# Two transformer blocks on one core: norms joined to the residual ahead of them and the dense stage behind them

## The chip, the core and the metric

One core of a Trainium2 chip runs the whole program. The metric is the time of one execution on the device, in microseconds (us). The five engines have an instruction stream each: TensorE (PE, its weight loads PEld), VectorE (DVE), ScalarE (ACT), GpSimd (POOL) and SyncE (SP, which here only issues loads). All numbers are f32, so a 128x128 by 128x512 matmul takes TensorE two passes, and the trace counts two instructions for it.

## The reference, cut to what matters

```python
def rmsnorm(x, g):
    y = x32 * lax.rsqrt(jnp.mean(x32 * x32, axis=-1, keepdims=True) + EPS)
    return (y * g.astype(jnp.float32)).astype(x.dtype)

def modulate(x, g, shift, scale):
    return rmsnorm(x, g) * (1 + scale) + shift
```

The first block (512 latent and 256 context tokens of width 1024) is: modulated norm, projections, a chunked state-space scan, its output times silu(z) and normed over 2048 features, windowed attention, a gated merge of both, `w_out`, and a feed-forward part with a depthwise convolution (`w_up`, `w_down`); then a final norm. The second block has four layers (SGU, RWKV, MLA, SGU). Each adds `gate * mixer(h)` to x, with `h = rms_norm(x) * (1 + scale) + shift`; the first two also update the context. MLA norms its ranks: `q = rms_norm(c_q, q_norm) @ w_uq`, and likewise `c_kv` for latent and context tokens.

## The kernel before

Features lie on the partitions, tokens along the free axis: x is 8 tiles of 128 features by 512 tokens (`A_XL`) and 8 by 256 (`A_XC`). Weights come tile by tile through two slots; SP issues the load of a tile as soon as TensorE has released its slot (`slot_used`), also across stages.

The program is a list of stages. `program` walks it on each engine: before stage n an engine waits until all four compute engines have finished stage n-1 (`eng.wait_ge(chip.stage_done, 4 * n)`, line 3814), then runs its own part. That is the barrier. POOL also clears the semaphores of every other stage there. `Joined` runs two stages as one, without a barrier; before, three norms are joined to the dense stage behind them (`norm_in` with `Xbc`, two layer norms with `SguValues`, one with the q projection).

`Norm` (line 643) works in four steps. ScalarE squares each tile (line 666). TensorE adds the squares over partitions and tiles with a matrix of ones (line 683), one matmul for each tile of 128 features, and then runs 8 filler matmuls (`keep_busy`, line 691; 3 where `norm.busy = 3`). ScalarE takes the root (line 669). VectorE takes the reciprocal (line 704) and scales each tile (line 707), and ScalarE adds the shift (line 675).

The stages around the change, in order (34 barriers in all):

- `GateZ` (line 1173): 16 products with `w_z`. ScalarE takes silu, VectorE multiplies y (line 1216) and then does a part of the modulation's products beside it (`SideModulation.reduce`, line 632, on weights `w_side` that POOL loads). `LoadContext` on SP waits for the stage barrier and loads the second block's context, ahead of the loads of `w_qkv`. Norm of y over 2048 features. `Attention` (line 1224): four projections into banks 0 to 3, then the values, then rotation and heads. `Merge` reads the normed y.
- `StrassenResidual` (line 1575): x += gate * (w @ y) with seven products of half-size blocks in place of eight, four passes of seven. `w_out1`, then a norm, then `FfnUp` (line 1691), which begins with sums of blocks of weights (`a_sum`) and of h (`b_sum`) on VectorE.
- `Residual` for `w_down` (line 1538, 8 steps of 22 matmuls), the final norm, the first layer's norm, `SguValues` (line 1876).
- `w_sgu_out`, norm, `RwkvFeatures` (line 2693), which needs differences of neighbouring tokens of the whole h before its first product.
- `w_rwkv_out`, norm, three projections to the MLA ranks (`Project`, line 2251, copies on line 2286), a norm of the ranks, `Mla` (line 2302).
- `w_mla_out`, norm, `SguValues`.

Of the kernel before, what the change touches and what calls it, by code (L numbers as in the profile page):

```python
# [20 lines left out]
P = 128  # L21
# [401 lines left out]
class Joined:  # L423


    def __init__(self, chip, first, make_second):
        self.first = first
        chip.joining = True
        self.second = make_second(first)
        chip.joining = False  # L430
        self.index = first.index

    def sync(self, sp):
        self.first.sync(sp)
        self.second.sync(sp)

    def tensor(self, pe):
        self.first.tensor(pe)
        self.second.tensor(pe)

    def scalar(self, act):
        self.first.scalar(act)
        self.second.scalar(act)

    def vector(self, dve):
        self.first.vector(dve)
        self.second.vector(dve)

    def gpsimd(self, pool):
        self.first.gpsimd(pool)  # L450
        self.second.gpsimd(pool)
# [191 lines left out]
class Norm(Stage):  # L643


    def __init__(self, chip, name, jobs, work):
        super().__init__(chip)
        self.jobs, self.work = jobs, work
        self.squared, self.summed, self.rooted, self.scaled, self.shifted = (
            chip.sem(f"{name}_{s}") for s in ("squared", "summed", "rooted", "scaled", "shifted"))  # L650
        self.busy = 8

    def places(self):

        at = self.work
        for n, job in enumerate(self.jobs):
            k, t = job["x"].shape[1:]
            yield job, n, self.chip.view(at, k, t), self.chip.view(at, t), self.chip.view(at + t, t), \
                self.chip.view(A_SMALL + 32 * n, k), k, t
            at += k * t  # L660

    def scalar(self, act):
        a = self.nc.scalar
        for job, n, squares, rms, inv, factor, k, t in self.places():
            for i in range(k):
                a.activation(squares[:, i], job["x"][:, i], ACT.Square).then_inc(self.squared, 1)  # L666
        for job, n, squares, rms, inv, factor, k, t in self.places():
            act.wait_ge(self.summed, n + 1)
            a.activation(rms, self.chip.bank(n, t), ACT.Sqrt, scale=1.0 / (k * P), bias=EPS).then_inc(self.rooted, 1)
        done = 0  # L670
        for job, n, squares, rms, inv, factor, k, t in self.places():
            if job.get("shift") is not None:
                for i in range(k):
                    act.wait_ge(self.scaled, done + i + 1)
                    a.activation(job["out"][:, i], job["out"][:, i], ACT.Identity, bias=job["shift"][:, i:i + 1]).then_inc(self.shifted, 1)
            done += k

    def tensor(self, pe):
        done = 0
        for job, n, squares, rms, inv, factor, k, t in self.places():  # L680
            for i in range(k):
                pe.wait_ge(self.squared, done + i + 1)
                last = self.nc.tensor.matmul(self.chip.bank(n, t), self.chip.const("ones"), squares[:, i], start=(i == 0), stop=(i == k - 1))  # L683
            last.then_inc(self.summed, 1)
            done += k
        self.keep_busy()

    def keep_busy(self):

        for i in range(self.busy):  # L690
            self.nc.tensor.matmul(self.chip.bank(7), self.chip.const("ones"), self.chip.view(A_CONST, 512), start=True, stop=True)

    def vector(self, dve):
        v = self.nc.vector
        for job, n, squares, rms, inv, factor, k, t in self.places():
# [3177 lines left out]
```

## Time and profile before

| what | us |
|---|---|
| median of 3 runs (5244.01 to 5247.77) | 5244.16 |
| profiled execution | 5238.18 |
| its span | 5236.4 |
| PE busy in it | 4717.6 (90%) |
| DVE busy | 2623.1 (50%) |
| ACT busy | 1226.9 (23%) |
| POOL busy | 661.0 (13%) |
| mean granted clock of TensorE | 0.954 |

The span is the time from the first to the last instruction of the profiled execution; 1.8 us of that execution lie around it. The granted clock is a share of TensorE's full 2.4 GHz. In a row of a timeline, "x16" counts the instructions that were merged, and the brackets give the engine's idle time ahead of it and what ended that.

### The profile page before, as it was taken

What the parts mean: (1) busy time and instruction counts of PE and PEld (TensorE: products, weight loads), DVE (VectorE), ACT (ScalarE), POOL (GpSimd) and SP (SyncE); (2) the same over time, 40 slices, a digit from 0 to 9 for tenths busy, and PEclk for the clock granted to TensorE, in tenths of its full rate; (3) what the DMA queues carried; (4) which work ended last, traced back from release to release, by engine and by line L of the source; (5) the groups of instructions that cost most, each with busy time, mean ns of one, the idle gap of its engine ahead of it and who ended that gap; (6) DMA issues with size and microseconds to landing.
All of it is one profiled execution on the core that took longest, in us unless ns stands there. A gap on an engine that the chain in (4) does not pass through costs nothing.

```text
span 5236.4 us, 72681 instructions
## 1 busy us (share of the span) xinstructions
PE 4717.6 (90%) x29212; PEld 3011.0 (58%) x29212; DVE 2623.1 (50%) x4628; ACT 1226.9 (23%) x2254; POOL 661.0 (13%) x894
## 2 busy tenths in 40 slices
PE   7987798989999989999989856899898999999998
PEld 3555645544578434555545545789644555455687
DVE  2457754655588222334476486455624444333465
ACT  2223312420011010111010164223112444301230
POOL 0014400000000000110000041655000000000000
PEclk9999999989999999999989966999999999999999
DMA  4322150034322211223112266344211001021222
GB/s 149 102 83 81 61 177 29 31 131 156 106 73 81 75 54 41 99 100 107 36 48 99 101 214 217 91 113 114 67 45 49 29 35 37 21 93 65 73 85 81
DMA packets 152504, 451.27 MB, mean 86 GB/s; under 512 B 73200, under 2 KB 73456, under 8 KB 130800
## 3 DMA queue, kind: packets, MB, share of 16 engines
q1 hardware_dynamic: 128464, 350.91, 19.8%
q0 software_dynamic: 22848, 92.29, 5.1%
q8 instruction: 233, 3.82, 0.3%
q10 hardware_dynamic: 864, 3.47, 0.2%
q14 instruction: 95, 0.78, 0.0%
HBM read 377.42 MB, written 69.21 MB: 85 GB/s over the span
## 4 chain that ended last, share of the span: by engine, by line
PE 60%; issue 10%; DVE 9%; PEld 8%; POOLq 5%; ACT 2%; DMA 2%; DVEq 2%; POOL 1%; PEldq 0%; SPq 0%; ACTq 0%
PE psum L389 44%; PEld psum L389 7%; PE psum L1906 5%; POOLq L2905 2%; POOLq L2903 2%; PE psum L2275 1%; PE psum L683 1%; PE psum L2463 1%; PE psum L2464 1%; DVE sbuf L1156 1%; DVE sbuf L704 1%; PE psum L2435 1%; PE psum L1094 1%; DVE sbuf L2610 1%; DVE sbuf L707 1%
## 5 line engine op out<-in xcount | busy, mean ns | idle before, releaser
L389 PE MATMUL psum<-sbuf 128*128 128x256 f32 (+3 forms) x9328 | 2938.9, 474 | 109.4 <-DVE sbuf L1657 32.7
L389 PEld LDWEIGHTS psum<-sbuf 128*128 128x128 f32 (+1 forms) x9328 | 1757.1, 190 | 1247.9 <-issue 915.1
L3515 PE MATMUL psum<-sbuf 64*64 64x64 f32 (+1 forms) x10752 | 425.9, 238 | 29.7 <-SPq L3424 18.1
L3515 PEld LDWEIGHTS psum<-sbuf 64*64 64x64 f32 x10752 | 412.2, 138 | 46.2 <-SPq L3424 19.8
L1906 PE MATMUL psum<-sbuf 128*128 128x512 f32 x640 | 280.1, 599 | 15.7 <-ACTq L1913 8.6
L632 DVE CUSTOM_DVE_ANT_0 sbuf<-sbuf 128x1024 f32<-128x1024 f32 x160 | 196.2, 1226 | 135.1 <-DMA sbuf<-w_side 99.7
L1906 PEld LDWEIGHTS psum<-sbuf 128*128 128x128 f32 x640 | 122.6, 192 | 173.1 <-issue 172.1
L1669 DVE SCALAR_TENSOR_TENSOR sbuf<-psum,sbuf 128x256 f32<-128x256 f32 (+2 forms) x288 | 125.9, 480 | 189.9 <-PE psum L389 184.8
L3640 ACT ACTIVATE sbuf<-psum 128x256 f32<-128x256 f32 (+3 forms) x384 | 128.5, 368 | 363.8 <-PE psum L3515 302.2
L666 ACT ACTIVATE sbuf<-sbuf 128x512 f32<-128x512 f32 (+1 forms) x114 | 53.0, 551 | 598.4 <-DVEq L3814 581.2
L2904 POOL TENSOR_TENSOR sbuf<-sbuf 96x30 f32<-96x30 f32 (+14 forms) x240 | 138.3, 576 | 50.9 <-issue 18.1
L622 POOL DMA_DIRECT2D sbuf<-w_side x128 | 68.4, 535 | 592.9 <-DVE sbuf L632 567.1
L1932 DVE TENSOR_TENSOR sbuf<-sbuf 128x512 f32<-128x512 f32 x40 | 27.8, 694 | 226.1 <-ACT sbuf L1922 226.1
L2902 POOL TENSOR_TENSOR sbuf<-sbuf 96x30 f32<-96x30 f32 (+14 forms) x240 | 131.0, 546 | 33.0 <-issue 0.9
L3745 DVE TENSOR_SCALAR sbuf<-psum,sbuf 128x64 f32<-128x64 f32 x192 | 45.7, 280 | 148.3 <-PE psum L3515 147.0
L1657 DVE TENSOR_TENSOR sbuf<-sbuf 128x1024 f32<-128x1024 f32 (+1 forms) x100 | 100.2, 1006 | 31.1 <-DMA sbuf<-w_sgu_out 12.2
L683 PE MATMUL psum<-sbuf 128*128 128x512 f32 (+1 forms) x228 | 94.0, 570 | 22.9 <-ACT sbuf L666 22.9
L2610 DVE TENSOR_REDUCE sbuf<-psum 128x1 f32<-128x768 f32 x64 | 61.2, 956 | 106.4 <-PE psum L2464 106.0
L589 POOL DMA_DIRECT2D sbuf<-cond_rows x4 | 2.4, 603 | 874.5 <-DVEq L3814 815.9
L2806 DVE TENSOR_TENSOR sbuf<-sbuf,psum 128x384 f32<-128x384 f32 x128 | 66.7, 553 | 78.5 <-PE psum L389 75.8
L720 DVE TENSOR_SCALAR sbuf<-sbuf 128x512 f32<-128x512 f32 (+1 forms) x68 | 36.3, 533 | 138.2 <-ACT sbuf L850 136.1
L2463 PE MATMUL psum<-sbuf 128*128 128x512 f32 (+1 forms) x256 | 104.4, 489 | 0.0
(329 smaller groups left out, 5244.5 us busy)
## 6 DMA issues: line engine op xcount, KB each, us to landing
sbuf<-w_side POOLq DMA_DIRECT2D x128, 512.0 KB, 3.9
sbuf<-w_sgu_uz SPq DMA_DIRECT2D x32, 1088.0 KB, 5.0
sbuf<-terms SPq DMA_DIRECT2D x115, 256.0 KB, 2.8
sbuf<-w_up SPq DMA_DIRECT2D x22, 1024.0 KB, 5.0
sbuf<-w_merge SPq DMA_DIRECT2D x8, 2560.0 KB, 8.9
sbuf<-w_mla_head SPq DMA_DIRECT2D x16, 1152.0 KB, 5.1
sbuf<-w_sgu_v SPq DMA_DIRECT2D x8, 2048.0 KB, 7.9
sbuf<-w_sgu_out SPq DMA_DIRECT2D x8, 2048.0 KB, 8.2
```

Of the source, the lines that this page charges most:

```text
L389: last = nc.tensor.matmul(out, w, x, start=(n == 0), stop=(n == len(pairs) - 1))
L632: last = v.tensor_tensor_reduce(junk, self.slot[b], self.rows[:, c], 1.0, 0.0, ALU.mult, ALU.add, self.sums[:, b, n:n + 1])
L683: last = self.nc.tensor.matmul(self.chip.bank(n, t), self.chip.const("ones"), squares[:, i], start=(i == 0), stop=(i == k - 1))
L1669: last = v.scalar_tensor_tensor(x[:, m], self.chip.bank(i)[:, cols], gates[sign][:, m:m + 1], x[:, m], ALU.mult, ALU.add)
L1906: last = self.nc.tensor.matmul(self.chip.bank(x % 4), h[:, k, at:at + P], w[:, k], start=(k == 0), stop=(k == KD - 1))
L2463: t.matmul(s[:, a:a + w], self.qn[u][:, q], self.kn[u][:, a:a + w], start=True, stop=False)
L2610: v.tensor_reduce(self.mx[:, n:n + 1], self.s_bank(n), AX.X, ALU.max)
L2902: engine.tensor_tensor(product, left, right, ALU.mult)
L2903: eng.drain()
L2904: engine.tensor_tensor(x[:, j + 1:BLK, 0:j], x[:, j + 1:BLK, 0:j], product, ALU.add)
L3515: last = t.matmul(out[hs], lhs[hs], rhs[hs], start=start, stop=stop)
L3640: copy = lambda to, of: a.activation(to, of, ACT.Copy)
```

## The change

`Joined` takes any number of stages. Six joined groups replace 21 stages: gate, context load, norm and attention; `w_out1`, norm and `FfnUp`; `w_down`, final norm, new context, layer norm and `SguValues`; `w_sgu_out`, norm and `RwkvFeatures`; `w_rwkv_out`, norm, the three projections and the norm of the ranks; `w_mla_out`, norm and `SguValues`. The number of barriers falls from 34 to 19.

A norm now has a host, the stage ahead of it, and its work is cut in rows (one tile of latent features, or one of latent and one of context). TensorE adds a row's squares between the host's products as soon as the row is final (`sum_row`); what is left comes behind them (`last_sums`), then 8 fillers. ScalarE squares a row when the host says it is done (`next_row`), after loading the root's table. The norm of y has no fillers, takes bank 3, and its last sums stand behind the attention's first projection. In front of `SguValues` the latent half is scaled in four blocks of 128 tokens. `few` keeps the squares in two buffers, where room is short. Two of the first weight sums of `FfnUp` stand between the scalings. The context load waits for the start of its stage, which is now the gate's.

```diff
@@ class Joined @@
-    def __init__(self, chip, first, make_second):
-        self.first = first
+    def __init__(self, chip, make):
+        self.index = chip.begin_stage()
         chip.joining = True
-        self.second = make_second(first)
+        self.parts = make()
         chip.joining = False
...
@@ class Norm @@
+    def next_row(self, act, r):
+        for n, m in self.rows[r]:
+            self.host.row_done(act, n, m)
+        if self.few and r >= 2:
+            act.wait_ge(self.taken, r - 1)
+        self.square_row(act, r, [self.jobs[n]["x"][:, m] for n, m in self.rows[r]])
+    def sum_row(self, pe, r):
...
+            pe.wait_ge(self.squared, at + 1)
...
+            last = self.nc.tensor.matmul(self.chip.bank(self.banks[n], t), self.chip.const("ones"), self.square(r, n, m),
+                                         start=first, stop=at == self.last[n])
...
+        if self.host:
+            a.activation(self.chip.view(A_SMALL + 500, 1), self.chip.const("ones")[:, 0:1], ACT.Sqrt)
+            for r in range(self.started, len(self.rows)):
+                self.next_row(act, r)
...
+    def pieces(self):
+        for n, (k, t) in enumerate(self.sizes):
+            blocks = self.blocks if n == 0 else 1
+            for b in range(blocks):
+                for i in range(k):
+                    yield n, self.jobs[n], i, slice(t // blocks * b, t // blocks * (b + 1)), i == 0
...
+        if not self.placed:
+            self.last_sums(pe)
+            self.keep_busy()
...
@@ class GateZ @@
                 products(self.nc, self.chip.bank(u), [(w[:, k], self.h[:, k]) for k in range(KD)]).then_inc(self.w.used(u), 1)
+                if 2 * i + u >= 2:
+                    self.norm.sum_row(pe, 2 * i + u - 2)
...
                 self.nc.scalar.activation(self.z[u], self.chip.bank(u), ACT.Silu).then_inc(self.activated, 1)
+                if 2 * i + u >= 1:
+                    self.norm.next_row(act, 2 * i + u - 1)
...
@@ class Attention @@
-        for n in range(4):
+        pe.wait_ge(self.gate.activated, KS + 1)
+        project(0, 0, 0)
+        self.norm.last_sums(pe)
+        pe.wait_ge(self.gate.activated, KS + 2)
+        for n in range(1, 4):
+            if n == 3:
+                pe.wait_ge(self.norm.rooted, 1)
+                pe.wait_ge(self.norm.scaled, 1)
             project(0, n, n)
...
         act.dma_start(self.mask, c.dram["win_mask"]).then_inc(self.tables_in, 16)
+        act.wait_ge(self.norm.scaled, 1)
         act.dma_start(self.wv.rearrange("p k m -> p (k m)"), c.dram["w_att_v"]).then_inc(self.wv_in, 16)
...
@@ class Residual @@
+                if self.norm and 2 * i + u >= 1:
+                    self.norm.sum_row(pe, 2 * i + u - 1)
...
@@ class StrassenResidual @@
+    ROWS = (4, 0, 5, 1, 6, 2, 7, 3)
+    def row_done(self, eng, n, m):
+        eng.wait_ge(self.added, 7 * (m % (KD // 2)) + (7 if m < KD // 2 else 6))
...
+                if self.norm and p == KD // 2 - 1 and i >= 1:
+                    if i == 1:
+                        pe.wait_ge(self.added, 7 * p + 1)
+                    self.norm.sum_row(pe, i - 1)
...
@@ class FfnUp @@
+                    if j == 0:
+                        pe.wait_ge(self.norm.shifted, self.HALF * (S.B_PLAIN[n][0] + 1))
...
+    def first_sums(self, dve, i):
+        if i == self.HALF - 1:
+            self.a_sum(dve, 0, 2)
+        if i == KD - 1:
+            self.a_sum(dve, 0, 5)
...
             first, second, op = S.B_SUMS[n]
+            dve.wait_ge(self.norm.shifted, KD)
...
@@ class SguValues @@
-                    if (i, u, t) == (0, 0, 0):
-                        pe.wait_ge(self.norm.shifted, k + 1)
+                    if (i, u) == (0, 0) and t < 4:
+                        pe.wait_ge(self.norm.shifted, KD * t + k + 1)
...
@@ class Project @@
+            if self.rank and self.row + 2 * i + u >= 1:
+                self.rank.sum_row(pe, self.row + 2 * i + u - 1)
...
@@ class RwkvFeatures @@
-        for h, at, n in self.parts:
+        for h, at, n in reversed(self.parts):
+            dve.wait_ge(self.norm.shifted, KD if n == TL else 2 * KD)
...
@@ block1, sgu_layer, rwkv_layer, mla_layer @@
+    def attention():
+        gate, load = GateZ(chip, side), LoadContext(chip)
+        norm = Norm(chip, "norm_ssd", [dict(x=y, out=y, gain=chip.vec("ssd_g"))], None, host=gate, by_host=KS - 2, started=KS - 1, banks=[3],
+                    few=dict(slots=[ATT, ATT + TL], roots=[ATT + 2 * TL]), turn=2, placed=True)
+        return [gate, load, norm, Attention(chip, gate, norm)]
...
+    def down():
+        residual = Residual(chip, "w_down", KF, lambda k: g[:, k], part(5, 0))
+        norm = Norm(chip, "norm_out", [dict(x=x_lat, out=x_lat, gain=chip.vec("final_g"))], FFN_G + KF * TL,
+                    rows=[[(0, m)] for m in range(KD)], host=residual, by_host=KD - 1, banks=[7], turn=2)
+        return [residual, norm, NewContext(chip, load)]
...
+    def projected():
+        stages = before()
...
+        return stages + [norm, q, kv, Project(chip, "w_mla_rope", 1, both, chip.view(KROPE, 1, T), previous=kv), rank]
```

TensorE around the end of the gate's products, before (L389 are products of a dense stage, L683 sums of squares, L691 fillers):

```order
L389 MATMUL psum<-sbuf 128x512 x128
L683 MATMUL psum<-sbuf 128x512 x16
L691 MATMUL psum<-sbuf 128x512 x8
L389 MATMUL psum<-sbuf 128x512 x24
L389 MATMUL psum<-sbuf 128x256 x56
```

and now (L714 sums of squares), from the sum behind the 13th of the 16 gate products on:

```order
L714 MATMUL psum<-sbuf 128x512
L389 MATMUL psum<-sbuf 128x512 x8
L714 MATMUL psum<-sbuf 128x512
L389 MATMUL psum<-sbuf 128x512 x8
L714 MATMUL psum<-sbuf 128x512
L389 MATMUL psum<-sbuf 128x512 x8
L714 MATMUL psum<-sbuf 128x512
L389 MATMUL psum<-sbuf 128x512 x8
L714 MATMUL psum<-sbuf 128x512 x2
L389 MATMUL psum<-sbuf 128x512 x16
L389 MATMUL psum<-sbuf 128x256 x56
```

The 16 sums stood in one block behind the gate. Now one follows each of the gate's products from the third on, and the last two follow the attention's first projection; the fillers are gone.

TensorE from `w_down` to the SGU values (L1906), before:

```order
L389 MATMUL psum<-sbuf 128x512 x176
L683 MATMUL psum<-sbuf 128x512 x8
L691 MATMUL psum<-sbuf 128x512 x8
L683 MATMUL psum<-sbuf 128x512 x8
L683 MATMUL psum<-sbuf 128x256 x8
L691 MATMUL psum<-sbuf 128x512 x3
L1906 MATMUL psum<-sbuf 128x512 x192
```

and now, from the sum behind the sixth step of `w_down` on (L761 fillers, L2043 values):

```order
L714 MATMUL psum<-sbuf 128x512
L389 MATMUL psum<-sbuf 128x512 x22
L714 MATMUL psum<-sbuf 128x512
L389 MATMUL psum<-sbuf 128x512 x22
L714 MATMUL psum<-sbuf 128x512 x2
L761 MATMUL psum<-sbuf 128x512 x8
L714 MATMUL psum<-sbuf 128x256 x8
L714 MATMUL psum<-sbuf 128x512 x8
L761 MATMUL psum<-sbuf 128x512 x8
L2043 MATMUL psum<-sbuf 128x512 x192
```

Of the final norm's eight sums six lie between the products, one behind the last one, and one waits for its result. The layer norm adds the context first, and has 8 fillers in place of 3.

TensorE from `w_rwkv_out` to the MLA ranks (projections are L2275), before:

```order
L389 MATMUL psum<-sbuf 128x384 x112
L683 MATMUL psum<-sbuf 128x512 x8
L683 MATMUL psum<-sbuf 128x256 x8
L691 MATMUL psum<-sbuf 128x512 x3
L2275 MATMUL psum<-sbuf 128x512 x56
L2275 MATMUL psum<-sbuf 128x256 x8
L2275 MATMUL psum<-sbuf 128x512 x8
L2275 MATMUL psum<-sbuf 128x256 x8
L2275 MATMUL psum<-sbuf 128x512 x8
L2275 MATMUL psum<-sbuf 128x256 x8
L683 MATMUL psum<-sbuf 128x512 x8
L683 MATMUL psum<-sbuf 128x256 x2
L691 MATMUL psum<-sbuf 128x512 x8
```

and now, from the first of the two `w_mla_kv` products on (projections are L2430):

```order
L2430 MATMUL psum<-sbuf 128x512 x8
L2430 MATMUL psum<-sbuf 128x256 x8
L714 MATMUL psum<-sbuf 128x512
L2430 MATMUL psum<-sbuf 128x512 x8
L2430 MATMUL psum<-sbuf 128x256 x8
L714 MATMUL psum<-sbuf 128x512
L714 MATMUL psum<-sbuf 128x256
L2430 MATMUL psum<-sbuf 128x512 x8
L2430 MATMUL psum<-sbuf 128x256 x8
L714 MATMUL psum<-sbuf 128x512
L714 MATMUL psum<-sbuf 128x256
L761 MATMUL psum<-sbuf 128x512 x8
```

The sums of the ranks' squares stand one product behind, and only the last row and the fillers follow the third projection.

## Rows read from the trace of the kernel before

**Rows 1.** The page, part 1: TensorE's and the other engines' busy time.

```profile
PE 4717.6 (90%) x29212; PEld 3011.0 (58%) x29212; DVE 2623.1 (50%) x4628; ACT 1226.9 (23%) x2254; POOL 661.0 (13%) x894
```

**Rows 2.** Stretches: us, length, busy of five engines (instructions), granted clock, DMA share, GB/s.

```profile
760.70:801.00 40.30, 23.47 (x49) 9.95 (x48) 20.40 (x29) 10.90 (x19) 0.10 (x1) 0.80 0.30 117
1430.80:1450.50 19.70, 14.02 (x33) 6.01 (x33) 10.24 (x13) 11.51 (x18) 0.00 (x0) 1.00 0.17 53
1890.00:1933.90 43.90, 29.77 (x70) 14.05 (x71) 23.58 (x31) 22.08 (x44) 0.00 (x0) 0.86 0.13 48
1933.90:1943.40 9.50, 9.49 (x17) 4.23 (x18) 0.00 (x0) 1.71 (x3) 0.00 (x0) 0.75 0.00 0
2628.70:2667.70 39.00, 17.52 (x50) 9.05 (x49) 29.37 (x32) 18.93 (x36) 0.00 (x0) 0.80 0.04 13
3837.20:3860.60 23.40, 13.22 (x39) 7.12 (x39) 14.65 (x22) 15.94 (x34) 0.00 (x0) 0.92 0.08 23
...
4770.00:4788.10 18.10, 9.72 (x22) 4.09 (x23) 9.40 (x11) 10.89 (x18) 0.00 (x0) 0.92 0.32 116
```

**Rows 3.** Timeline, ACT: the gate's last two silus and the fourth projection's eviction.

```profile
753.88 0.60 ACT L1207 ACTIVATE sbuf<-psum 128x512 f32<-128x512 f32 x1 [6.28 <-PE psum L389]
760.76 0.60 ACT L1207 ACTIVATE sbuf<-psum 128x512 f32<-128x512 f32 x1 [6.28 <-PE psum L389]
...
827.62 0.38 ACT L1374 ACTIVATE sbuf<-psum 128x256 f32<-128x256 f32 x1 [2.87 <-PE psum L389]
```

**Rows 4.** Timeline, gate stage: a silu, a reduction and the multiply behind it.

```profile
725.89 1.23 DVE L632 CUSTOM_DVE_ANT_0 psum<-sbuf 128x1024 f32<-128x1024 f32 x1 [0.64 <-DMA sbuf<-w_side]
726.36 0.60 ACT L1207 ACTIVATE sbuf<-psum 128x512 f32<-128x512 f32 x1 [6.28 <-PE psum L389]
...
728.76 0.69 DVE L1216 TENSOR_TENSOR sbuf<-sbuf 128x512 f32<-128x512 f32 x1
```

**Rows 5.** The tile `w_qkv`: its four loads.

```profile
DMA to landing us min/median/max: 6.4/7.5/11.4
```

**Rows 6.** Timeline, PE: the layer norm's sums and the first SGU values.

```profile
1909.56 13.18 PE L683 MATMUL psum<-sbuf 128*128 128x512 f32 x32 [3.94 <-ACT sbuf L666]
...
1933.91 31.40 PE L1906 MATMUL psum<-sbuf 128*128 128x512 f32 x67 [8.59 <-ACTq L1913]
```

**Rows 7.** Timeline, same place: reciprocals and scalings on DVE, first eviction on ACT.

```profile
1899.42 3.35 DVE L704 RECIPROCAL sbuf<-sbuf 128x512 f32<-128x512 f32 x1 [8.26 <-ACT sbuf L669]
1902.85 5.39 DVE L707 SCALAR_TENSOR_TENSOR sbuf<-sbuf 128x512 f32<-128x512 f32 x8
...
1928.68 1.75 DVE L704 RECIPROCAL sbuf<-sbuf 128x256 f32<-128x256 f32 x1
...
1943.42 0.60 ACT L1922 ACTIVATE sbuf<-psum 128x512 f32<-128x512 f32 x1 [7.79 <-PE psum L1906]
```

**Rows 8.** Timeline, start of `FfnUp`: first sums of h, second weight tile.

```profile
1450.87 3.49 DVE L1785 TENSOR_TENSOR sbuf<-sbuf 128x1024 f32<-128x1024 f32 x3
...
1464.80 5.42 PE L389 MATMUL psum<-sbuf 128*128 128x256 f32 x24 [0.26 <-issue]
```

**Rows 9.** Timeline, RWKV layer: sums, reciprocal, first vector work, first product.

```profile
2630.20 10.61 PE L683 MATMUL psum<-sbuf 128*128 128x512 f32 x32 [1.48 <-ACT sbuf L666]
...
2638.17 3.35 DVE L704 RECIPROCAL sbuf<-sbuf 128x512 f32<-128x512 f32 x1 [8.34 <-ACT sbuf L669]
...
2652.69 2.28 DVE L2776 TENSOR_TENSOR sbuf<-sbuf 128x2032 f32<-128x2032 f32 x1 [0.70 <-ACTq L3814]
...
2667.68 2.90 PE L2830 MATMUL psum<-sbuf 128*128 128x512 f32 x4 [20.00 <-DVE sbuf L2760]
```

**Rows 10.** Timeline, norm of the ranks: first reciprocal, and MLA's first load.

```profile
3945.26 3.35 DVE L704 RECIPROCAL sbuf<-sbuf 128x512 f32<-128x512 f32 x1 [6.51 <-ACT sbuf L669]
...
3960.25 0.34 ACTq L2488 DMA_DIRECT2D sbuf<-rope_mla  x1
```

**Rows 11.** Timeline, ACT: first eviction of the last layer's SGU values.

```profile
4797.30 0.60 ACT L1922 ACTIVATE sbuf<-psum 128x512 f32<-128x512 f32 x1 [7.28 <-PE psum L1906]
```

More of the change, by code:

```diff
@@ new lines, in row_done, with square, sums_done, square_row @@
+    def row_done(self, eng, n, m):
+        if n == 0:
+            eng.wait_ge(self.scaled, m + 1)
+    def square(self, row, n, m):
+        if self.few:
+            k, t = self.sizes[n]
+            return self.chip.view(self.few["slots"][row % 2] + (0, self.sizes[0][1])[n], t)
+        return self.squares[n][:, m]
+    def sums_done(self, eng, n):
+        eng.wait_ge(self.summed, 1 + sum(last < self.last[n] for last in self.last))
+    def square_row(self, act, r, sources):
+        for (n, m), x in zip(self.rows[r], sources):
+            self.nc.scalar.activation(self.square(r, n, m), x, ACT.Square).then_inc(self.squared, 1)
@@ L662, in scalar @@
     def scalar(self, act):
         a = self.nc.scalar
[L664 to L669, printed above, removed]
+        if self.host:
+            a.activation(self.chip.view(A_SMALL + 500, 1), self.chip.const("ones")[:, 0:1], ACT.Sqrt)
+            for r in range(self.started, len(self.rows)):
+                self.next_row(act, r)
+        elif self.by_host == 0:
+            for r, row in enumerate(self.rows):
+                self.square_row(act, r, [self.jobs[n]["x"][:, m] for n, m in row])
@@ L670, in scalar @@
+        for n, (k, t) in enumerate(self.sizes):
+            self.sums_done(act, n)
+            a.activation(self.rms[n], self.chip.bank(self.banks[n], t), ACT.Sqrt, scale=1.0 / (k * P), bias=EPS).then_inc(self.rooted, 1)
         done = 0
-        for job, n, squares, rms, inv, factor, k, t in self.places():
+        for n, job, i, cols, _ in self.pieces():
+            done += 1
             if job.get("shift") is not None:
+                act.wait_ge(self.scaled, done)
+                a.activation(job["out"][:, i, cols], job["out"][:, i, cols], ACT.Identity, bias=job["shift"][:, i:i + 1]).then_inc(self.shifted, 1)
@@ L678, in tensor @@
     def tensor(self, pe):
[L679 to L686, printed above, removed]
+        if not self.placed:
+            self.last_sums(pe)
+            self.keep_busy()
@@ L1854, in block1, with ffn, inputs @@
     g = chip.view(FFN_G, KF, TL)
-    return [
+    def ffn():
+        out1 = StrassenResidual(chip, "w_out1", merged, [(x_lat, part(2, 0), TL)], A_WORK, A_HL)
+        norm = Norm(chip, "norm_ffn", [dict(x=x_lat, out=h_lat, gain=g2, scale=part(4, 0), shift=part(3, 0))], A_WORK + KD // 2 * 5 * TL // 2,
+                    rows=[[(0, m)] for m in out1.ROWS], host=out1, by_host=6, banks=[7], turn=1)
+        return [out1, norm, FfnUp(chip, norm)]
+    def inputs():
+        norm = Norm(chip, "norm_in", [job_lat, job_ctx], A_WORK)
+        return [norm, Xbc(chip, side, norm)]
@@ L1873 @@
+    return stages, down
 SGU_V = A_WORK
```

223 lines of the change are left out of this document (140 added, 83 removed).

## The prediction, before the changed kernel was run

> **What bounds the kernel now.** I read the page first: TensorE is busy 90% of the span [rows 1]. So only its idle stretches, its slow stretches and its filler products can be saved. I then cut the span at the places where the changed kernel joins stages, one stretch for each, from the end of the last product ahead of a norm to the first one behind it [rows 2]. The reader is to see two things there: each stretch is long (18 to 44 us), and the granted clock is under 1 in most of them and in the 9.5 us behind one (0.75), so the first products after a norm run partly at 1.2 GHz. The timeline of the engine that ends a stretch gives the times inside it [rows 3, 6 to 11]. I call the end of the last product E. A product of eight 128x512 matmuls takes 6.88 us at full clock, the step between two evictions [rows 3], so 0.86 us for one matmul and 0.43 for 128x256. Eight filler matmuls of `keep_busy` take 6.9.
>
> **What the change does, in general.** The sums of squares (one 0.86 us matmul per 128 rows of features) are not removed. Most move into the product loop ahead, where TensorE has no gap, so each costs its full time there; I charge all of them to the path. What goes is the barrier, the wait for squares, the idle time behind the fillers and the slow restart. Fillers: eight in every late norm, against three before in three norms.
>
> **1. Gate, norm, attention.** Before, the fourth of the attention's projections is evicted at 827.62, 66.9 us after E = 760.7 [rows 2, 3]; between lie vector reductions that finish late, 16 sums, 8 fillers, a wait for the scalings and a slow restart (clock 0.80 over the stretch). Now the projections need only free banks; the norm of y is read two stages later. Path: 16 sums 13.8, projections 3 x 6.88 + 3.44 = 24.1, eviction 0.3: 38.2. **Gain 28.7.** The last projection waits for the root (bank 3), which comes about 13 us before it is needed. The reciprocal and 16 scalings (3.4 and 16 x 0.67 = 14.1 us by the rates of [rows 7]) lie beside projections and values. If that cover were missing, VectorE's rotation would be late; it has some 20 us of spare, since the values follow. Behind the new ScalarE wait for `scaled` stand the load of the value weights and the four copies; the load is issued some 12 us before it is used. On SP the context load no longer waits for the gate's end and holds up nothing behind it; on POOL only the clearing of semaphores between stages falls away.
>
> **2. w_out1, norm, w_up.** Now, from E: 8 sums 6.9 (the last row's squares come within the two sums ahead of it), root 0.9, reciprocal 3.4, eight scalings 5.4 [rows 7] and two weight sums 1.4 between them, shift 0.7: the first sum of h starts at E + 18.7, against 1450.87 - 1430.8 = 20.1 [rows 8]. Then 13.9 us passed until the second weight tile's products [rows 8], 12.1 of them seven products of 1.73. Two of these (3.5) now run before the sum; the rest waits for VectorE's sums. This is worth 0 to 3.5; I take 3.0, since VectorE's sums take only 7.6 of the 13.9. **Gain 4.4**, bounds 1 to 6.
>
> **3. w_down, norm, norm, SGU values.** Before, the first values are evicted at 1943.42, 53.4 us after E = 1890.0 [rows 7]. Now: eight sums with a short wait for the last row 7.8, 8 fillers 6.9, 8 context sums 3.4, 8 latent sums 6.9, 8 fillers 6.9: 31.9. The chain beside it (root, reciprocal, scaling, squares, root, reciprocal of 128 columns, first shift) is ready at 27.5, so the fillers set the time. Reciprocals took 3.35 for 512 and 1.75 for 256 columns [rows 7]; for 128 I take 0.9, between 0.8 and 1.75, hidden either way. Plus 6.88 + 0.2: 39.0. **Gain 14.4**, bounds 11 to 16.5.
>
> **4. w_sgu_out, norm, RWKV features.** Here the first product needs the whole norm and 14 us of vector work. Before, the reciprocal starts at E + 9.5 and the first product is 29.5 later [rows 9]. Now all 16 sums are on the path: the latent ones end at 9.9, root 0.9, reciprocal at 10.9, then the same chain less one barrier, 0.7 [rows 9]: 39.7, against 39.0. **Loss 0.7**, bounds -3 to +1.5. The row's 20.00 us of idle time stays.
>
> **5. w_rwkv_out, norm, three projections, norm, MLA.** Before, MLA's first load is issued at 3960.25, 123.1 us after E = 3837.2 [rows 10]. Now: 16 sums 10.3, fillers 6.9, so q starts at 17.2 (its input is ready at 15.7; before 23.4 [rows 2] and slow). Projections 72.2 (six of 6.88, three of 10.32), seven rank rows 6.5: 95.9. Then copies and roots 1.8, and 15.0 from the first reciprocal to the barrier [rows 10]: 112.7. **Gain 10.3**, bounds 8 to 12.5.
>
> **6. w_mla_out, norm, SGU values.** Before, first eviction at 4797.30, 27.3 after E = 4770.0 [rows 11]. Now 8 sums 6.9, fillers 6.9, product 6.88, 0.2: 20.9. **Gain 6.4**, bounds 4 to 8.
>
> **The sum.** 28.7 + 4.4 + 14.4 - 0.7 + 10.3 + 6.4 = 63.5 us. The profiled execution took 5238.2 (span 5236.4); that gives 5174.7. The median of the runs shown is 6.0 above it, so I predict 5180.7. A 0.2% step, 10.5 us, is what a measurement of this kernel can tell from no change.
>
> **A rule weighed.** The restarts credited above are some 2 us each: behind the SGU norm, after 3.94 and 8.59 us of idle time [rows 6], the clock was 0.75 for 9.5 us [rows 2], and the first eviction came 2.4 us later than 6.88 + 0.2. About as much stands in parts 1 (2.3), 5 (1.7) and 6 (2.1); without them the gain would be 8.5 smaller. The Trainium skill, page TensorE: Matmul & The Clock Gate, Part 1, says that "the default state is throttled, and activity releases the throttle". By that rule the added fillers are worth having; by the rows they cost up to 4.2 us each where the input is ready first (part 6: input at 9.6, fillers end at 13.8). I go by the rows: fillers are charged in full, and the restart is free behind them.
>
> **Rivals.**
> - **Each hosted row costs more than its matmul.** 65 sums stand alone between accumulations into other banks. At a pass's seam TensorE stood 0.26 us idle [rows 8]. At that price for each: 17 us, gain 46.5, 5198. For it: every such sum has a wait of its own. Against: the squares are there long before, and 16 that follow each other took 10.6 us, 0.3 over 8 x (0.86 + 0.43) [rows 9].
> - **Loads lose their cover.** The attention's first weights (1536 KB, 6.4 to 11.4 us to landing [rows 5]) were loaded beside the norm. Now they have 8.6 us, with a 1 MB context load just ahead. At worst 3 us there, and a few us more where w_sgu_v's second tile comes late: 5185.
> - **The gate loop turns into a chain, slower than before.** ScalarE now squares row k-1 behind silu k and waits for VectorE's multiply, which stands behind a reduction that waits for w_side. If that multiply comes over 5.7 us after its silu (ScalarE's 6.28 us of idle time [rows 3] less a 0.55 us square), the next silu and then TensorE stall. With all else gained it needs over 4.5 us more in each of 14 steps to pass the time before; with 5 us it would be 5251. The largest lag seen was 2.4 us (728.76 behind 726.36 [rows 4]). So it is far from its point, and longer steps ease the loads. The page Perfetto Trace Analysis of the Trainium skill, Per-instruction lifecycle, calls ACT and DVE strict FIFO; by that rule nothing behind the waiting square can pass it, and the trace agrees in that VectorE's multiply starts only behind the reductions, with no idle time of its own [rows 4].
> - **The joined stages end no sooner.** If another engine ended them (VectorE in 2 to 4), only part 1 would count: 5215.
>
> **How the numbers follow.** Forecast 0.77 (5170 to 5192), costly rows 0.11, loads 0.05, no sooner 0.02, no effect within 0.2% 0.03, chain 0.02. All of the bounds at their worst give a gain of 47, at their best 75: 5169 to 5197. I widen both ends by a few us for the median and the costly rows: 5166 to 5202. Faster by over 0.2%: 0.95; within: 0.03; slower: 0.02.
>
> **What would show it.** The fourth projection evicted 27 us behind the gate's last product (38.2 less the 13 sums that now stand ahead of it); first SGU evictions without a slow pass (steps of 6.88 from the start); the 20 us wait of the RWKV features still there, some 2 us longer; MLA's first load 113 us after E, hosted sums included. Wrong would be: idle TensorE inside the gate loop, sums of over 1 us each, a wait on w_qkv, or a granted clock under 1 behind the fillers.

## The result, and the profile after

The changed kernel takes 5190.27 us in the median of four runs (5182.09 to 5194.39), the kernel before, beside it, 5244.97 (5244.01 to 5247.77). The ratio is 0.9897, with a 95% interval of 0.9882 to 0.9911: 54.7 us faster, where 63.5 was forecast. The profiled execution took 5182.09, 56.1 less than the profiled one of before. The forecast of 5180.7 (5166 to 5202) holds the time, but the sum behind it is not as good as that looks: two of its terms did not come, and gains outside the change's own places stood in for them.

The page's first part, after, answers to [rows 1]:

```profile
span 5180.3 us, 72699 instructions
PE 4703.1 (91%) x29226; PEld 3006.8 (58%) x29226; DVE 2631.4 (51%) x4682; ACT 1240.5 (24%) x2309; POOL 660.3 (13%) x894
```

To see which part gave what, I measured the same stretch in both traces, from one instruction to another that exist in both kernels (us):

| part | from, to | before | after | gain | forecast |
|---|---|---|---|---|---|
| 1 | first silu of the gate, attention's swaps | 191.0 | 162.0 | 29.0 | 28.7 |
| 2 | w_out1's first weight sum, w_down's last addition (5.2 of hosted sums taken off) | 512.0 | 506.3 | 5.7 | 4.4 |
| 3 | w_down's last addition, first eviction of the values (the same 5.2 put on) | 53.4 | 53.4 | 0.0 | 14.4 |
| 4 | w_sgu_out's first weight sum, first product of the features | 189.3 | 189.3 | 0.0 | -0.7 |
| 5 | w_rwkv_out's first weight sum, MLA's first load | 199.6 | 189.7 | 9.9 | 10.3 |
| 6 | w_mla_out's first weight sum, first eviction of the values | 128.8 | 131.1 | -2.3 | 6.4 |

These add up to 42.3. The other 13.8 lie where the change does nothing: 5.0 ahead of the gate's first product, 5.6 from the RWKV features to w_rwkv_out, 1.5 behind the first SGU values, 1.7 behind MLA's load and behind the last values.

The 5.2 us are six hosted sums of 0.86. They now run ahead of w_down's last addition, and the forecast counts them in part 3.

**Part 1** is as forecast. TensorE's timeline of after shows the sum behind the gate's last product, the attention's first projection, the last two sums, and the other projections and values, 144 instructions (72 matmuls) in one run up to the swaps. A product and a hosted sum take 7.74 us together (766.68 to 774.42), 6.88 and 0.86, with no idle time. The fourth projection is evicted at 793.56, 26.9 us behind the gate's last product; 27 was forecast.

```profile
766.68 1.02 PE L714 MATMUL psum<-sbuf 128*128 128x512 f32 x2
767.54 7.04 PE L389 MATMUL psum<-sbuf 128*128 128x512 f32 x16
774.42 1.88 PE L714 MATMUL psum<-sbuf 128*128 128x512 f32 x4
776.13 38.56 PE L389 MATMUL psum<-sbuf 128*128 128x512 f32 x144
814.53 2.74 PE L1378 MATMUL psum<-sbuf 128*128 128x512 f32 x6
```

**Parts 4 and 5**: the first product of the features still waits for VectorE, 22.09 us where it was 20.00 [rows 9]; the q projection starts directly behind the fillers, at full speed (granted clock 1.00 from 3797 to 3813).

```profile
2626.50 12.29 PE L2996 MATMUL psum<-sbuf 128*128 128x512 f32 x32 [22.09 <-DVE sbuf L2925]
...
3801.34 7.03 PE L761 MATMUL psum<-sbuf 128*128 128x512 f32 x16
3808.20 13.92 PE L2430 MATMUL psum<-sbuf 128*128 128x512 f32 x32
```

**Part 3** is where the forecast fails. TensorE's timeline of after around the norm (fillers of norm_out, sixteen sums, fillers of the layer's norm, values), against [rows 6]:

```profile
1857.90 7.03 PE L761 MATMUL psum<-sbuf 128*128 128x512 f32 x16
1864.76 10.51 PE L714 MATMUL psum<-sbuf 128*128 128x256 f32 x32
1875.11 7.03 PE L761 MATMUL psum<-sbuf 128*128 128x512 f32 x16
1893.68 31.50 PE L2043 MATMUL psum<-sbuf 128*128 128x512 f32 x66 [11.55 <-issue]
```

and ScalarE's over the same stretch (roots, shifts of four latent blocks and of the context, the table of Gelu, evictions), against [rows 7]:

```profile
1875.31 0.87 ACT L733 ACTIVATE sbuf<-psum 128x512 f32<-128x512 f32 x2 [7.10 <-PE psum L714]
1877.35 2.45 ACT L739 ACTIVATE sbuf<-sbuf 128x128 f32<-128x128 f32 x8 [1.17 <-DVE sbuf L777]
...
1886.73 2.45 ACT L739 ACTIVATE sbuf<-sbuf 128x128 f32<-128x128 f32 x8 [0.68 <-DVE sbuf L777]
1890.79 3.30 ACT L739 ACTIVATE sbuf<-sbuf 128x256 f32<-128x256 f32 x8 [1.61 <-DVE sbuf L777]
1894.11 1.28 ACT L2059 ACT_TABLE_LOAD   x1
1903.72 0.60 ACT L2059 ACTIVATE sbuf<-psum 128x512 f32<-128x512 f32 x1 [8.32 <-PE psum L2043]
1910.60 0.60 ACT L2059 ACTIVATE sbuf<-psum 128x512 f32<-128x512 f32 x1 [6.28 <-PE psum L2043]
```

There are three times to see. The first block's shifts run from 1877.35, the fillers end at 1882.1, both as forecast. But the first product starts at 1893.68, and that is when ScalarE's last shift starts, not when its first is done (eight in 3.30 us from 1890.79, the last of them from 1893.60). The blocks were made so that TensorE could begin after one of them, and it began after all. Then the first eviction comes 10.04 us later, where a product of 6.88 and 0.2 to its eviction make 7.08. The windows view, TensorE alone (start and end, length, busy, granted clock), shows why: the clock was granted in full behind the fillers, fell in the idle time, and came back only at 1900:

```profile
1880.00:1884.00 4.00, 2.14 (x5) 1.00 0.00 0
1884.00:1888.00 4.00, 0.00 (x0) 0.73 0.00 0
1888.00:1892.00 4.00, 0.00 (x0) 0.50 0.00 0
1892.00:1896.00 4.00, 2.31 (x3) 0.50 0.00 0
1896.00:1900.00 4.00, 4.00 (x6) 0.56 0.00 0
1900.00:1904.00 4.00, 4.00 (x11) 1.00 0.00 0
```

Part 6 has the same pattern, with 6.55 us of idle time (the last shifts run from 4730.88 to 4733.32, the first eviction comes at 4741.55):

```profile
4719.26 7.03 PE L761 MATMUL psum<-sbuf 128*128 128x512 f32 x16
4732.84 22.43 PE L2043 MATMUL psum<-sbuf 128*128 128x512 f32 x48 [6.55 <-issue]
```

**The theory** to test is in the code. `SguValues.tensor` waits for `activated >= x + 1` ahead of product x, and `SguValues.scalar` begins with `act.sem_inc(self.activated, 4)`, the credit for four free banks. Inside one joined stage that line stands in ScalarE's stream behind all the norm's shifts. The source view shows when this instruction ran, in after (line 2050) and in before (line 1913):

```profile
L2050 ACTq EVENT_SEMAPHORE  x2: 17/17/17, 1893.6 to 4732.7; - x2
```

```profile
L1913 ACTq EVENT_SEMAPHORE  x2: 17/17/17, 1933.8 to 4788.0; - x2
```

Each of the four stands 0.1 us ahead of the first product of its place (1893.68 and 4732.84 after, 1933.91 and 4788.11 before). **Rivals**: the idle time is TensorE's own (the view says "issue"), or the places are bound by the fillers.

### The profile page after: what moved, and what is told of

Read it like the earlier page. It is cut to its first block, busy times and chain, and to the rows that moved or that the text cites. A ratio compares the mean times of both kernels' runs of the same rounds, so it can differ in the third digit from the quotient of the medians.

```text
span 5180.3 us, 72699 instructions
## 1 busy us (share of the span) xinstructions
PE 4703.1 (91%) x29226; PEld 3006.8 (58%) x29226; DVE 2631.4 (51%) x4682; ACT 1240.5 (24%) x2309; POOL 660.3 (13%) x894
## 4 chain that ended last, share of the span: by engine, by line
PE 66%; issue 10%; DVE 8%; POOLq 5%; PEld 4%; DVEq 2%; ACT 2%; DMA 2%; POOL 1%; PEldq 0%; SPq 0%; ACTq 0%
PE psum L389 49%; PE psum L2043 5%; PEld psum L389 4%; POOLq L3071 2%; POOLq L3069 2%; PE psum L714 2%; PE psum L2430 1%; DVE sbuf L1229 1%; PE psum L2622 1%; PE psum L2621 1%; PE psum L2593 1%; DVE sbuf L2768 1%; PE psum L1167 1%; PE psum L761 1%; PE psum L1391 1%
## 5 line engine op out<-in xcount | busy, mean ns | idle before, releaser
L389 PE MATMUL psum<-sbuf 128*128 128x256 f32 (+3 forms) x9328 | 2937.9, 473 | 100.2 <-DVE sbuf L1764 32.6
L389 PEld LDWEIGHTS psum<-sbuf 128*128 128x128 f32 (+1 forms) x9328 | 1754.3, 190 | 1236.0 <-issue 905.3
L3681 PE MATMUL psum<-sbuf 64*64 64x64 f32 (+1 forms) x10752 | 427.4, 238 | 28.7 <-SPq L3590 18.0
L2043 PE MATMUL psum<-sbuf 128*128 128x512 f32 x640 | 280.1, 600 | 18.1 <-issue 18.1
L2043 PEld LDWEIGHTS psum<-sbuf 128*128 128x128 f32 x640 | 122.7, 192 | 175.6 <-issue 174.5
## 6 DMA issues: line engine op xcount, KB each, us to landing
sbuf<-w_side POOLq DMA_DIRECT2D x128, 512.0 KB, 3.9
```

The source lines that it names most:

```text
L389: last = nc.tensor.matmul(out, w, x, start=(n == 0), stop=(n == len(pairs) - 1))
L2043: last = self.nc.tensor.matmul(self.chip.bank(x % 4), h[:, k, at:at + P], w[:, k], start=(k == 0), stop=(k == KD - 1))
L3681: last = t.matmul(out[hs], lhs[hs], rhs[hs], start=start, stop=stop)
```

## The experiments

For the first ones I read one distance in each trace: from the start of the latent rows' root to the third eviction of the values. From the third on, all of them are in step at 6.88 us.

| kernel | place 3 | place 6 |
|---|---|---|
| before | 37.9 | 32.6 |
| changed | 42.2 | 35.9 |
| e9 the changed kernel again | 42.2 | 36.8 |
| e4 places 3 and 6 apart | 38.0 | 33.4 |
| e2 one block | 38.6 | 32.2 |
| e1 no credit | 27.5 | 27.5 |
| e3 no credit, no fillers | 25.2 | 25.2 |
| e6 no credit, three fillers | 23.5 | 23.5 |
| e7 before, no credit | 26.7 | 28.3 |

**e1, the credit taken away.** The four banks are free by the first shift, since the roots that read the norm's sums stand ahead of it on ScalarE.

```diff
-                pe.wait_ge(self.activated, 2 * self.nt * i + x + 1)
+                if 2 * self.nt * i + x >= 4:
+                    pe.wait_ge(self.activated, 2 * self.nt * i + x - 3)
...
-        act.sem_inc(self.activated, 4)
...
-                dve.wait_ge(self.activated, 2 * self.nt * i + u * self.nt + t + 5)
+                dve.wait_ge(self.activated, 2 * self.nt * i + u * self.nt + t + 1)
```

> The changed kernel, in both value stages of the SGU layers without the credit of four banks that ScalarE gives (the first four products wait for no evacuation; every later wait asks for four less). Theory: TensorE's first product waits for that credit, which stands in ScalarE's stream behind all shifts of the norm (last one 1894.1 in the first of the two stages, 4733.3 in the second), and not for the fillers (ends 1882.1 and 4726.3). Then the first product starts behind the fillers, 11.6 and 6.6 us earlier, and its slow first pass (10.0 and 8.7 us to the first eviction where the next steps are 6.88) shortens by up to 3.2 and 1.8: 18 to 23 us less than the changed kernel in all, some 0.985 of the time of the kernel before. Rival: the idle time in front of the products is TensorE's own (code, queue) and would stay; then the time stays at 0.990 of the kernel before.

It took 5166.19 us, ratio 0.9856 (0.9837 to 0.9875). The products follow the fillers with no gap, and ScalarE finds two results ready when it comes out of its shifts:

```profile
1886.73 7.03 PE L761 MATMUL psum<-sbuf 128*128 128x512 f32 x16
1893.60 21.66 PE L2044 MATMUL psum<-sbuf 128*128 128x512 f32 x50
```

```profile
1902.43 3.31 ACT L739 ACTIVATE sbuf<-sbuf 128x256 f32<-128x256 f32 x8 [1.61 <-DVE sbuf L777]
1905.75 1.28 ACT L2058 ACT_TABLE_LOAD   x1
1907.05 1.11 ACT L2058 ACTIVATE sbuf<-psum 128x512 f32<-128x512 f32 x2
1914.44 0.60 ACT L2058 ACTIVATE sbuf<-psum 128x512 f32<-128x512 f32 x1 [6.28 <-PE psum L2044]
```

14.7 us at place 3 and 8.4 at place 6, 23.1 in all: the credit's theory, at the top of its range. The rival "TensorE's own idle time" is out. The fillers were not the bound of the changed kernel; here they are.

**e2, one block of 512 columns, credit kept** (`blocks=1` in both norms, the waits on `shifted` to match).

> The changed kernel with the norm of both SGU value stages scaled and shifted in one block of 512 columns instead of four of 128; the credit stays behind the shifts. Theory (credit): the last shift comes earlier, since 4 blocks take 4 x 3.13 = 12.5 us and one block 3.35 + 5.39 = 8.7 by the reciprocal and the scalings of 512 columns: 3 to 4 us less at each of the two places, 6 to 8 us less than the changed kernel. Rival (the prediction's: blocks let the products begin early, and the fillers set their start): the first shifted row comes some 2.4 us later (reciprocal 3.35 instead of 0.95), still about when the fillers end: no change, or up to 3 us more.

5183.62 us, 0.9886 (0.9869 to 0.9902); the median alone would not tell it from the changed kernel. The distances do: 3.6 and 3.7 us less (place 6 itself repeats within 0.9). With the credit where it is, cutting the scaling into blocks cost time at both places.

**e3, no credit and no fillers** (`norm.busy = 0` for both SGU norms, on top of e1).

> The kernel without the credit, and also without the eight filler products at the end of the norm in both SGU value stages. Theory: the fillers (7.03 us, 1875.1 to 1882.1) hold TensorE beyond the first shift of block 0 (about 1877.7), so the products start 4.4 us earlier at each place, 6 to 9 us less than the kernel without the credit alone. Rival: without them the granted clock falls for the first products and takes back 3 us or more at each place, so no change or slower.

5159.04 us, 0.9846 (0.9829 to 0.9864). It gave 2.3 us at each place, between theory and rival: both act. The products start 4.1 us earlier behind the root, and the clock that falls in 2.63 us of idle time takes 1.8 back. TensorE's row, and the windows over it:

```profile
1888.32 22.14 PE L2045 MATMUL psum<-sbuf 128*128 128x512 f32 x47 [2.63 <-ACT sbuf L739]
```

```profile
1888.00:1892.00 4.00, 3.68 (x6) 1.69 (x7) 3.92 (x14) 3.32 (x12) 0.00 (x0) 0.68 0.00 0
1892.00:1896.00 4.00, 4.00 (x9) 1.66 (x8) 3.93 (x13) 3.32 (x12) 0.00 (x0) 0.89 0.00 0
1896.00:1900.00 4.00, 4.00 (x11) 1.72 (x10) 3.93 (x10) 2.92 (x10) 0.00 (x0) 1.00 0.00 0
```

(busy time of PE, weight loads, VectorE, ScalarE and GpSimd, then the granted clock.)

**e4, parts 3 and 6 undone.** The stages stand apart as before; `norm_out` and the layers' norms square and sum on their own.

```diff
-        stages = before()
...
-        return stages + [norm, SguValues(chip, layer, nt, norm)]
+        norm = norm2(chip, layer, A_WORK, banks=[0, 1] if nt == 6 else [0])
+        norm.busy = 3
+        return [norm, SguValues(chip, layer, nt, norm)]
...
-    stages = [Joined(chip, values), SguMix(chip, layer, j, nt, side) if nt == 6 else SguMixSeven(chip, layer, j)]
+    stages = before() + [Joined(chip, values), SguMix(chip, layer, j, nt, side) if nt == 6 else SguMixSeven(chip, layer, j)]
```

> The changed kernel with its parts 3 and 6 undone: w_down, norm_out, the context's return and the norm with SguValues are stages of their own again in the first place, w_mla_out and the norm with SguValues in the second, with 3 fillers and one block; the rest as changed. The prediction's terms (14.4 and 6.4) would make it 20.8 us slower than the changed kernel, 0.994 of the kernel before. What the anchors in the trace of the changed kernel say (+0.6 and -2.1 for the two places) would leave it within 3 us of the changed kernel, 0.989 to 0.990.

5179.07 us, 0.9877 (0.9857 to 0.9897): no slower than the changed kernel. The 20.8 us of the two terms are refuted; as built, joining at these two places brought nothing that can be measured. The stretches of the table say the same: with the joins undone part 3 takes 53.8 us and part 6 131.3, against 53.4 and 131.1 with them. That e4's time is even 8 to 11 us under the two medians of the changed kernel does not come from these places: from the features' first product to w_rwkv_out it took 1079.1 us, against 1087.4.

**e5, part 1 undone.** Gate, load, norm and attention are four stages again:

```diff
-                if 2 * i + u >= 2:
-                    self.norm.sum_row(pe, 2 * i + u - 2)
...
-        pe.wait_ge(self.gate.activated, KS + 1)
-        project(0, 0, 0)
-        self.norm.last_sums(pe)
...
-        (gated := Joined(chip, attention)),
+        *(gated := attention()),
```

> The changed kernel with its part 1 undone: the gate, the context's load, the norm and the attention are stages of their own again, no square or sum is hosted by the gate, and the attention's tensor program has its old order; the rest as changed. Theory (the prediction's part 1): 28.7 us slower than the changed kernel, with some 33 us from the gate's last product to the attention's swaps back in the trace (before 848.59 - 760.7 = 87.9); 0.995 of the kernel before. Rival (the gate's step of 7.74 us instead of 6.88 costs more than its sum, or the stretches behind gain by themselves): under 25 us.

5226.39 us, 0.9971 (0.9961 to 0.9980). The stretch from the first silu to the swaps is 192.3 us against 162.0: 30.3, as expected, with the idle times of before back in TensorE's timeline:

```profile
772.43 17.07 PE L714 MATMUL psum<-sbuf 128*128 128x512 f32 x32 [9.34 <-ACT sbuf L697]
789.34 7.03 PE L761 MATMUL psum<-sbuf 128*128 128x512 f32 x16
804.44 47.94 PE L389 MATMUL psum<-sbuf 128*128 128x512 f32 x160 [8.08 <-DVEq L3977]
```

But the medians stand 36 to 40 apart. Of what is left over, most lies in a stage that e5 does not touch, the RWKV terms (224.5 us against 214.8); e9 to e11 follow that up.

**e6, e1 with three fillers** (`norm.busy = 3` in both SGU norms).

> The kernel without the credit, with three fillers instead of eight in both SGU norms. Without the credit and with eight, the third evacuation comes 27.5 us behind the last root; with none 25.2, TensorE being idle for 2.63 us and the granted clock under 1 for the next 8 us. Three fillers take 2.6 us. Theory: they fill just the gap until the first shift, the clock stays at 1.00 and five fillers of 0.86 are saved: 23.2 us at both places, 8.6 us less than with eight fillers, 4 less than with none. Rival: the clock falls all the same or the first product waits for the shifts: 25 us, no better than with none.

5153.83 us, 0.9834 (0.9817 to 0.9851). 23.5 us at both places, 4.0 less than with eight fillers and 1.7 less than with none. Three fillers fill the wait for the first shift exactly, and the windows from 1880 to 1896 all show a clock of 1.00:

```profile
1883.34 2.74 PE L761 MATMUL psum<-sbuf 128*128 128x512 f32 x6
1886.13 19.16 PE L2045 MATMUL psum<-sbuf 128*128 128x512 f32 x44
```

**e7, the kernel before without the credit** (e1's edit, on before).

> The kernel before, with only the credit of both SGU value stages taken away. Theory (the credit is what the first product waits for there too, as the idle time of 8.59 us in front of it said): the first product starts with the first shifted row, at 1924.9 and 4784.0 instead of 1933.91 and 4788.11, and the third evacuation comes 8 to 12 us and 4 to 6 us earlier: 12 to 18 us in all, 0.997 of the time before. Rival (the wait was for the first shifts or the change of stage): no change.

5220.05 us, 0.9958 (0.9941 to 0.9974). 11.2 us at place 3 and 4.2 at place 6, 15.4 in all (the times say 14 to 31, by the interval of the ratio). So the wait of [rows 6], 8.59 us on "ACTq L1913", was this credit, and it could be read before the change: line 1913 is `act.sem_inc(self.activated, 4)`. At place 6 the timeline of before named the shifts instead (7.07 us, line 675), though the credit stood behind them; without it 3.17 us of waiting for the first shift are left.

```profile
1923.09 2.74 PE L691 MATMUL psum<-sbuf 128*128 128x512 f32 x6
1925.66 24.68 PE L1907 MATMUL psum<-sbuf 128*128 128x512 f32 x57
```

**e8, e6 without the fillers of norm_out** (`norm.busy = 0` in `down`).

> The kernel with three fillers, and none at the end of norm_out, whose eight stand between its last sum (1857.9) and the sums of the next norm's context rows. The squares of those rows are there from 1859.0 on and those of the latent rows from 1863.6 on, one every 0.66 us. Theory: the sixteen sums run from 1859 to about 1870.5 instead of 1875.3, 4 to 5 us less in that place and no filler needed, as TensorE is idle for 1 us at a time. Rival: the sums without fillers ahead run at the lower clock, which takes the 4 us back: no change.

5149.40 us, 0.9817 (0.9800 to 0.9834), the fastest of all: 37 to 41 us under the two medians of the changed kernel. From norm_out's root to the next norm's it is 12.7 us (1863.56 to 1876.28) where it was 17.2: 4.5, as expected. The sums run at their full speed behind two short gaps:

```profile
1864.70 3.70 PE L714 MATMUL psum<-sbuf 128*128 128x256 f32 x16 [1.18 <-ACT sbuf L697]
1869.09 7.15 PE L714 MATMUL psum<-sbuf 128*128 128x512 f32 x16 [0.69 <-ACT sbuf L697]
```

**e9, e10, e11: the stretch that nobody changed.** The terms are measured from the stage's first 64x512 product to its first 64x64 one. e9 is the changed kernel again; e10 and e11 have 0 and 16 instead of 8 fillers ahead of the RWKV features, where TensorE waits anyway.

> The changed kernel as it is, again, beside the two next ones. What it is for: the stretch of the RWKV terms (from the first 64x512 product to the first 64x64 one) took 220.8, 224.5 and 222.5 us in the three kernels without part 1 and 209.4 to 214.8 us in the seven with it, though no instruction of it differs; TensorE is idle there with no wait that the profile shows for 29 to 34 us in the first three, 6 to 20 us in the others. If that hangs on the program (where the stage's code stands in TensorE's stream), the same kernel gives the same value again: 214.8 within 1, with about 20 us of such idle time. If it is chance from run to run, it lies anywhere in 209 to 225.

> The changed kernel without the eight fillers in front of the RWKV features, where TensorE then waits 22 us for VectorE, so they hide; eight matmuls fewer stand ahead of the stage of the terms in TensorE's stream, and nothing in that stage changes. If its unexplained idle time hangs on where its code stands, the stretch of the terms moves off 214.8 by more than 1.5 us, and the idle time without a wait with it; if it hangs on part 1 in some other way, it stays at 214.8 within 1. The features' first passes and the rest stay as they are, but for a clock that may fall at 2597 already: up to 1 us more there.

> The same with sixteen fillers there, 14.1 us that still hide in the wait of 22 us. As before: position in the stream moves the stretch of the terms off 214.8 by more than 1.5 us, another cause leaves it. TensorE's idle time in front of the features falls from 22.1 to about 15 us, and if its two passes of 12.3 us (eight matmuls of 128x512 and others at the lower clock) gain nothing from that, the length of the idle time does not matter once the clock has fallen.

| kernel | time, ratio | terms, us | TensorE idle there on "issue" |
|---|---|---|---|
| e10 (0 fillers) | 5186.45, 0.9886 | 210.9 | 10 |
| changed, first time | 5190.27, 0.9897 | 214.8 | 20 |
| e9 (8, the same kernel) | 5186.71, 0.9885 | 215.5 | 21 |
| e11 (16 fillers) | 5194.60, 0.9904 | 222.6 | 33 |
| before | | 220.8 | 29 |

The same kernel repeats its value to 0.7 us. Eight filler matmuls more or less, in another stage, at a place where they hide, move it by 4.6 and 7.1 us. The waits view of TensorE over the terms, e10 and then e11 (us in total, times, longest):

```profile
PE psum L3244 <- DVE sbuf L3393: 21.9, 8, 5.0
...
PE psum L3271 <- issue: 7.3, 2, 4.0
PE psum L3297 <- issue: 2.4, 1, 2.4
```

```profile
PE psum L3297 <- issue: 18.3, 4, 5.4
PE psum L3271 <- issue: 14.7, 4, 4.9
...
PE psum L3244 <- DVE sbuf L3393: 9.9, 8, 1.9
```

There are stops of 2 to 5 us in TensorE's stream for which the profile names no wait. Where they fall among the stage's instructions depends on how many instructions stand ahead; some positions are covered by the wait for VectorE (which grows from 9.9 to 21.9 as they shrink) and some are not. All thirteen profiles fall in line with that:

| matmul instructions ahead of the terms | terms, us |
|---|---|
| 9994 | 209.4 (e8) |
| 10004 | 210.2 (e3), 210.9 (e10) |
| 10010 | 211.1 (e4), 212.6 (e6) |
| 10020 | 213.3 (e2), 214.5 (e1), 214.8 (changed), 215.5 (e9) |
| 10026 | 220.8 (before), 222.5 (e7) |
| 10036 | 222.6 (e11), 224.5 (e5) |

So position is shown to be a cause, and nothing else of part 1 is needed to explain why the terms moved with it: undoing it (e5) puts back 16 filler instructions, as many as e11 adds, with nearly the same value.

The traces also say what the stops are. In the thirteen profiles there are 68 of them over 1.5 us long. Count TensorE's matmuls, weight loads and waits from the start: every stop stands at instruction 21185 or 21186, or at a multiple of 256 behind it. And every stop ends 0.7 to 1.6 us after a packet of 16 KB has landed on the queue that carries instructions:

```profile
q8 instruction: 233, 3.82, 0.3%
```

(packets, MB, share of the DMA engines.) TensorE stands still there until a block of its own instructions has come. This is read from thirteen traces; only the position was varied. The features' first pass took 12.27, 12.29 and 12.28 us behind 29, 22 and 15 us of idle time: once the clock had fallen, the length of the wait did not matter.

## Why the prediction was right and wrong

- **Part 1**, 28.7: right, 29.0 by the traces and 30.3 by undoing it. The gate's step is 7.74 us, no idle time inside it, and the projections follow in one run. The rival of the chained gate loop is out; so are that of costly hosted sums (0.86 us and no seam) and, at this place, that of the loads: `w_qkv` landed in 6.4 to 7.9 us, and no product waited for it.
- **Part 2**, 4.4: 5.7 in the changed kernel, 4.0 in e4, which has part 2 too. Right in size. With gains in parts 2 and 5, the rival that the joined stages end no sooner is out.
- **Part 3**, 14.4: wrong, it gave 0.0. The step that failed is "so the fillers set the time". Both of its times were good, but they were the wrong two: a third condition, the credit of banks that ScalarE gives behind all its shifts, came at 1893.6. That cost 11.55 us of idle time and 3.0 of slow restart (10.04 against 7.08). The prediction quoted the row that showed it, 8.59 us on ScalarE's queue [rows 6], and used it only as an idle time before a restart. Blocks make more shifts, and so a later credit: e2 gains 7.3 us by undoing them. With the credit gone, the fillers do set the time (e1), as the prediction had it.
- **Part 4**, -0.7: 0.0. The wait of 20.00 us stayed and grew to 22.09, as forecast.
- **Part 5**, 10.3: 9.9. Right, and it shows the same mechanism from the other side. In before, the three projections began with such a credit too (`act.sem_inc(self.copied, 2)`, line 2280), and q waited for it behind the shifts:

```profile
3860.61 43.09 PE L2275 MATMUL psum<-sbuf 128*128 128x512 f32 x96 [8.59 <-ACTq L2280]
```

That credit ran at 3860.5. The changed kernel's `Project` has none: its first products wait for the norm's shifts alone, as e1 later makes the values do. So here the input and the fillers were the whole condition, as the prediction had it. The prediction doesn't name this difference between parts 5 and 3, and no run puts the credit back here.
- **Part 6**, 6.4: wrong, -2.3, by the same step: 6.55 us of idle time and a slow restart of 1.6 (8.71 against 7.08), 8.2 in all. Of the -2.3 itself some 2 us may be scatter: e4, with this join undone, took 131.3 us too, where before took 128.8.
- **The sum.** The change's own places gave 42.3, not 63.5; parts 3 and 6 account for 23.1 of the difference, which is what e1 brings back (23.1). Outside them stood 13.8 that no term had. 5.0 of it lie ahead of the gate and are mostly chance (that first stretch was 652.5 us in this profile, 656.6 in e9's, 657.6 before), 5.6 go with the RWKV terms, where six matmul instructions fewer stand ahead than before. Hence the time was close by offsetting errors.
- **The rule weighed.** I went by the rows and charged the fillers in full. The truth lies between. Without fillers the clock falls in 2.63 us of idle time and costs 1.7 us (e3 against e6); with eight, 4.1 us are spent beyond the first shift (e1); three cost nothing and keep the clock (e6). The Trainium skill, page TensorE: Matmul & The Clock Gate, Part 1, says that activity releases the throttle; this trace agrees (0.68 behind the gap in e3, 1.00 with fillers in e6). But the rule gives no reason for more fillers than the wait is long. That the restart would be free behind fillers held only where the product followed them; behind 11.55 us of idle time the product started at a clock of 0.50 in spite of eight fillers.

## What to carry to other kernels

A credit for free buffers is an instruction like any other: it stands in its engine's stream behind whatever was joined ahead of it, and the source view shows when it ran. When stages are merged, list for the first instruction of the consumer every semaphore that it waits for, and find for each the place of its increment in the other engine's order; the last one sets the start, and it need not be the data. Fillers should be as long as the wait that they cover, and no longer. And to attribute a change of one per cent, compare stretches between the same instructions in both traces; the total also holds stretches that moved for other reasons.

## What was not expected of the hardware

A stretch of 215 us, with the same instructions in it, took from 209.4 to 224.5 us in thirteen profiles of twelve programs, and 214.8 and 215.5 in two profiles of one program. Eight hidden matmuls more or less in an earlier stage were enough to move it (210.9, 215.5, 222.6). TensorE's stops inside it stand at fixed places of its stream, a multiple of 256 instructions apart, and end 0.7 to 1.6 us after 16 KB of instructions have landed. Differences of some 8 us between two versions of this kernel can come with that alone, on medians too: e10 and e11 differ by 8.2 us.
